# Two attention mixers of a float32 transformer stack: attention steps ahead of the weight splits, and a new close of the output projection

## Time and profile before

| What | Value |
|---|---|
| Median of three runs | 1328.12 us (1325.83 to 1328.39) |
| The profiled execution's own time | 1326.24 us |
| Its span, first to last instruction | 1324.4 us |
| TensorE matmul busy | 1219.8 us, 92% |
| TensorE weight load busy | 1071.9 us, 81% |
| VectorE busy | 847.3 us, 64% |
| ScalarE busy | 574.4 us, 43% |
| GpSimd busy | 44.6 us, 3% |
| Mean granted TensorE clock | 0.939 of full |
| Loaded from memory | 243.06 MB, 187 GB/s over the span |

### The profile page before, as it was taken

One profiled execution on the slowest core, in us unless ns is written; L12 is line 12 of the kernel. 1 busy time (PEld: TensorE's weight loads), 2 busy tenths in 40 slices (PEclk: granted clock), 3 DMA queues, 4 the chain that ended last, 5 costly groups with the idle time before them and its releaser, 6 DMA issues.

```text
span 1324.4 us, 18386 instructions
## 1 busy us (share of the span) xinstructions
PE 1219.8 (92%) x7598; PEld 1071.9 (81%) x7598; DVE 847.3 (64%) x1276; ACT 574.4 (43%) x837; POOL 44.6 (3%) x86
## 2 busy tenths in 40 slices
PE   4989998999999988789999957999999899899997
PEld 3984776899998867579999847999988697899996
DVE  5662544587777766668777765977776445655554
ACT  5302231554444544455444455444446443744442
POOL 1010000000000000000000000000001100000000
PEclk9998556999999998899999978999999999899999
DMA  7933010488776423238877603977755432265530
GB/s 286 205 122 128 35 63 30 150 306 323 281 278 223 187 96 128 96 122 321 332 278 278 217 28 157 363 282 280 283 190 193 141 141 99 99 236 186 185 139 32
DMA packets 35746, 248.96 MB, mean 188 GB/s; under 512 B 4272, under 2 KB 4288, under 8 KB 6608
## 3 DMA queue, kind: packets, MB, share of 16 engines
q1 hardware_dynamic: 26352, 189.13, 38.3%
q0 software_dynamic: 9168, 57.56, 12.7%
q10 hardware_dynamic: 144, 1.11, 0.2%
HBM read 243.06 MB, written 4.19 MB: 187 GB/s over the span
## 4 chain that ended last, share of the span: by engine, by line
PE 81%; DVE 11%; ACT 4%; issue 2%; DMA 1%; DVEq 0%; SPq 0%; ACTq 0%
PE bank L1143 68%; DVE wlo L598 3%; PE bank L1318 2%; ACT whi L366 1%; PE bank L1502 1%; PE bank L1332 1%; DMA raw<-in_stream 1%; PE bank L1374 1%; DVE x L616 1%; DVE work L614 1%; PE bank L1221 1%; DVE ul L643 1%; PE bank L1385 1%; PE bank L1339 1%; PE bank L1341 1%
## 5 line engine op out<-in xcount | busy, mean ns | idle before, releaser
L598 DVE TENSOR_TENSOR wlo<-raw,whi 128x2048 fp32r<-128x2048 f32 x175 | 398.7, 2283 | 133.1 <-ACT whi L366 133.0
L1143 PE MATMUL bank<-uh,whi 128*128 128x256 f32 x1280 | 370.6, 289 | 2.9 <-DVE ul L643 2.9
L1143 PE MATMUL bank<-ul,whi 128*128 128x256 f32 x1280 | 363.6, 284 | 0.0
L1143 PE MATMUL bank<-uh,wlo 128*128 128x256 f32 x1280 | 363.5, 284 | 0.0
L366 ACT ACTIVATE whi<-raw 128x2048 fp32r<-128x2048 f32 x175 | 332.4, 1906 | 71.3 <-PE bank L1143 62.3
L1143 PEld LDWEIGHTS bank<-uh,whi 128*128 128x128 f32 x1280 | 246.9, 193 | 11.0 <-issue 8.9
L1143 PEld LDWEIGHTS bank<-ul,whi 128*128 128x128 f32 x1280 | 247.0, 193 | 4.7 <-issue 2.6
L1143 PEld LDWEIGHTS bank<-uh,wlo 128*128 128x128 f32 x1280 | 246.8, 193 | 0.0
L1143 PE MATMUL bank<-whi,hh 128*128 128x512 f32 x544 | 214.9, 395 | 0.0
L1143 PE MATMUL bank<-wlo,hh 128*128 128x512 f32 x544 | 212.9, 391 | 0.0
L1143 PE MATMUL bank<-whi,hl 128*128 128x512 f32 x544 | 212.2, 390 | 0.0
(11 more groups left out here) (229 smaller groups left out, 1157.8 us busy)
## 6 DMA issues: line engine op xcount, KB each, us to landing
raw<-in_stream SPq DMA_DIRECT2D x178, 1024.0 KB, 4.9
qk<-in_w_mod POOLq DMA_DIRECT2D x48, 1024.0 KB, 6.0
bias_rows<-PT POOLq DMA_DIRECT2D x1, 3072.0 KB, 36.3
u<-bias_rows POOLq DMA_DIRECT2D x16, 128.0 KB, 2.5
con<-in_con ACTq DMA_DIRECT2D x1, 1083.5 KB, 6.9
x<-in_x SPq DMA_DIRECT2D x2, 512.0 KB, 8.3
vo<-in_fin_g POOLq DMA_DIRECT2D x2, 512.0 KB, 4.3
out_y<-vo SPq DMA_DIRECT2D x2, 512.0 KB, 2.6
```

The costliest lines, as they stand in the source:

```text
L598: nc.vector.tensor_tensor(wlo[:, c % RING, 0:w], raw[:, raw_index(c) % RING, 0:w], whi[:, c % RING, 0:w].bitcast(fp32), ALU.subtract).then ...
L1143: ins = mm(out, st, mv, start=start and i == 0, stop=stop and i == 2, skip_group_check=True)
```

## The change

- The step tables are now separate for the two phases, and most steps sit in other quarters. Phase d has one turn for each pair and a table `JOIN_AT` for `combine`.
- On ScalarE, in both phases, `hi_upto` moves from q = 0, ahead of the attention work, to q = 1, behind it.
- In phase d the copy of the turned block to `PT` moves from VectorE to ScalarE, always into PT[:, 0].
- The value chunks 6 and 7 are no longer run as one: each takes both tiles in its own turn (`rows_of_values`), waits only for its own weights and raises `used` at its end.
- In `project_beside`, chunk 14 runs tile 0 with its steps 0 and 1, then the steps 2 and 3 without matmuls between; then chunk 15 closes tile 0, chunk 14 runs tile 1, `norm(e, 0)`, and chunk 15 closes tile 1.

The tables:

```diff
+SCORE_AT = {"d": {(4, 3): 0, (5, 2): 1, (6, 3): 2, (7, 2): 3, (10, 3): 4, (11, 1): 5, (12, 3): 6, (13, 1): 7},
+            "b": {(4, 1): 0, (4, 3): 1, (6, 1): 2, (6, 3): 3, (10, 1): 4, (10, 3): 5, (12, 1): 6, (12, 3): 7}}
+JOIN_AT = {(5, 3): 0, (6, 2): 1, (7, 3): 2, (8, 2): 3, (11, 2): 4, (12, 0): 5, (13, 2): 6, (14, 0): 7}
+TURN_AT = {"d": {(6, 1): (0, 0), (7, 0): (1, 0), (8, 1): (2, 0), (9, 0): (3, 0),
+                 (11, 3): (4, 0), (12, 1): (5, 0), (13, 3): (6, 0), (14, 1): (7, 0)},
+           "b": {(5, 1): (0, 0), (5, 2): (0, 1), (5, 3): (1, 0), (6, 0): (1, 1), (7, 1): (2, 0), (7, 2): (2, 1),
+                 (7, 3): (3, 0), (8, 0): (3, 1), (11, 1): (4, 0), (11, 2): (4, 1), (11, 3): (5, 0), (12, 0): (5, 1),
+                 (13, 1): (6, 0), (13, 2): (6, 1), (13, 3): (7, 0), (14, 0): (7, 1)}}
+VALUE_AT = {"d": {(6, 3): 0, (7, 2): 1, (9, 0): 2, (9, 2): 3, (12, 0): 4, (12, 2): 5, (14, 0): 6, (14, 2): 7},
+            "b": {(5, 3): 0, (6, 1): 1, (7, 3): 2, (8, 1): 3, (11, 3): 4, (12, 1): 5, (13, 3): 6, (14, 1): 7}}
+OUT_AT = {"d": {(8, 1): 0, (10, 1): 1, (13, 2): 2, (14, 3): 3},
+          "b": {(6, 3): 0, (8, 3): 1, (12, 3): 2, (14, 3): 3}}
```

ScalarE in phase d, and behind the second "..." in phase b:

```diff
             for i, q in QUARTERS:
-                if q == 0:
-                    if i and i <= 12 and MIXER[i - 1][0] == "v" and MIXER[i - 1][2] == 1:
-                        value_copies(MIXER[i - 1][1], 0, DIFF + i - 1, d_v)
-                    hi_upto(min(DIFF + i + 3, MLP1 + 1))
+                if q == 0 and 1 <= i <= 12 and MIXER[i - 1][0] == "v" and MIXER[i - 1][2] == 1:
+                    value_copies(MIXER[i - 1][1], 0, DIFF + i - 1, d_v)
+                if (i, q) in TURN_AT["d"]:
+                    p = TURN_AT["d"][i, q][0]
+                    act.wait_ge(s_tr["d"], p + 1)
+                    if p >= 1:
+                        act.wait_ge(s_pv["d"], p)
+                    nc.scalar.activation(PT[:, 0, :], bank[5][:, 0:384], ACT.Copy).then_inc(s_pt["d"], 1)
...
+                if q == 1:
+                    hi_upto(min(DIFF + i + 3, MLP1 + 1))
...
-                if q == 0:
+                if (i, q) in SCORE_AT["b"]:
+                    pair_exps("b", SCORE_AT["b"][i, q])
+                if (i, q) in OUT_AT["b"]:
+                    pair_upper(2, OUT_AT["b"][i, q], one)
+                if q == 1:
                     hi_upto(min(MOBA + i + 3, MLP3 + 1))
```

VectorE in phase d:

```diff
-                if (i, q) in TURN_AT and TURN_AT[i, q][1] == 0:
-                    turned_copy("d", *TURN_AT[i, q])
+                if (i, q) in JOIN_AT:
+                    combine(JOIN_AT[i, q])
...
-                if (i, q - 2) in SCORE_AT or (i - 1, q + 2) in SCORE_AT:
-                    combine(SCORE_AT.get((i, q - 2), SCORE_AT.get((i - 1, q + 2))))
```

TensorE, in `project_beside` and in the loops over `MIXER`:

```diff
-                for c in range(3):
+                for c in range(2):
                     pe.wait_ge(lo_ready, m0 + c + 1)
                     pe.wait_ge(ol_ready, 4 * r + c + 1)
                     add_rows(m0 + c, e, *parts(c), c == 0, False, steps=lambda q: steps(c, q))
+                pe.wait_ge(lo_ready, m0 + 3)
+                pe.wait_ge(ol_ready, 4 * r + 3)
+                add_rows(m0 + 2, e, *parts(2), False, False, (0,), steps=lambda q: steps(2, q))
+
+                for q in (2, 3):
+                    steps(2, q)
                 pe.wait_ge(lo_ready, m0 + 4)
                 pe.wait_ge(ol_ready, 4 * r + 4)
-                add_rows(m0 + 3, e, *parts(3), False, True)
+                add_rows(m0 + 3, e, *parts(3), False, True, (0,))
+                add_rows(m0 + 2, e, *parts(2), False, False, (1,))
                 norm(e, 0)
+                add_rows(m0 + 3, e, *parts(3), False, True, (1,))
...
+            def rows_of_values(m, g, steps):
+
+                pe.wait_ge(lo_ready, m + 1)
+                for t in range(NT):
+                    ins = half_values(m, g, t, None, lambda t, q: steps(2 * t + q % 2))
+                ins.then_inc(used, 1)
...
-                elif kind == "v" and k == 0:
-                    pe.wait_ge(d_add, 3)
-                    both_halves(DIFF + i, None, lambda t, q, i=i: (beside("d", 1, i + t)(q), dswap(i + t, q)))
+                elif kind == "v" and j == 1:
+                    if k == 0:
+                        pe.wait_ge(d_add, 3)
+                    rows_of_values(DIFF + i, k, steps)
```

More of the change, by code:

```diff
@@ L498, in value_copies @@
                 for t in range(NT):
-                    if t == 0:
-                        act.wait_ge(v_ps, base + h + 1)
+                    if t == 0 and h == 0:
+                        act.wait_ge(v_ps, base + 1)
                     else:
@@ L565, in _ @@
                     elif k == 1:
-                        value_copies(j, 2, MOBA + i - 1, b_v)
+                        value_copies(j, 1, MOBA + i - 1, b_v)
                         if i == 2:
                             spread_copy(3, cb, 6)
-                if q == 0:
+                if (i, q) in SCORE_AT["b"]:
[3 more added lines that the diff above has]
+                if q == 1:
                     hi_upto(min(MOBA + i + 3, MLP3 + 1))
[L571 to L574, removed]
             act.wait_ge(mod_ready, 3)
@@ L735, in turned_copy @@
             def turned_copy(ph, p, c):
-                n = p if ph == "d" else 2 * p + c
+                n = 2 * p + c
                 dve.wait_ge(s_tr[ph], n + 1)
@@ L1043, in _ @@
                     rope_sum(qk[:, 2 * j:2 * j + 2, :], bank[k], 2, r).then_inc(d_add, 1)
[L1044 to L1051 removed]
+                if (i, q) in SCORE_AT["d"]:
+                    pair_maxima("d", SCORE_AT["d"][i, q])
+                if (i, q) in JOIN_AT:
+                    combine(JOIN_AT[i, q])
+                if (i, q) in VALUE_AT["d"] and VALUE_AT["d"][i, q] % 2:
+                    sub_norm(VALUE_AT["d"][i, q] // 2)
+                if (i, q) in OUT_AT["d"]:
+                    pair_lower(1, OUT_AT["d"][i, q], lam[:, 6:7])
                 if q == 1:
                     lo_upto(min(DIFF + i + 3, MLP1 + 1))
[L1054 to L1055 removed]
             add_and_norm(3)
@@ L1103, in _ @@
             for i, q in QUARTERS:
[L1104 to L1109, removed]
+                if (i, q) in TURN_AT["b"]:
+                    turned_copy("b", *TURN_AT["b"][i, q])
+                if (i, q) in SCORE_AT["b"]:
+                    pair_maxima("b", SCORE_AT["b"][i, q])
+                if (i, q) in VALUE_AT["b"] and VALUE_AT["b"][i, q] % 2:
+                    j = VALUE_AT["b"][i, q] // 2
                     dve.wait_ge(s_exp["b"], 4 * j + 4)
@@ L1118, in _ @@
                     ins.then_inc(o_sc, 1)
-                if (i, q) in OUT_AT:
-                    pair_lower(2, OUT_AT[i, q], one)
+                if (i, q) in OUT_AT["b"]:
+                    pair_lower(2, OUT_AT["b"][i, q], one)
                 if q == 1:
@@ L1416, in steps @@
                 def steps(q):
[L1417 to L1424, removed]
+                    if (i, q) in VALUE_AT[ph]:
+                        pair_values(ph, r, VALUE_AT[ph][i, q])
+                    if (i, q) in TURN_AT[ph]:
+                        pair_turn(ph, *TURN_AT[ph][i, q])
+                    if (i, q) in SCORE_AT[ph]:
+                        pair_scores(ph, SCORE_AT[ph][i, q])
+                    if (i, q) in OUT_AT[ph]:
+                        pair_out(r, OUT_AT[ph][i, q])
                 return steps
@@ L1579, in both_halves @@
                     for g in range(2):
-                        ins = half_values(m + g, g, t, None if e is None else ul_no(e, t), steps)
+                        ins = half_values(m + g, g, t, ul_no(e, t))
                         if t == 1:
@@ L1584, in both_halves @@
                             ins.then_inc(v_ps, 1)
-                        if e is not None and t == 0 and g == 0:
+                        if t == 0 and g == 0:
                             norm(e, 1)
@@ L1645, in _ @@
                     spread_col(mod[:, 64:72], 6)
-                elif kind == "v" and k == 0:
-                    pe.wait_ge(b_copied, 3)
-                    both_halves(MOBA + i, None, lambda t, q, i=i: beside("b", 2, i + t)(q))
+                elif kind == "v" and j == 1:
+                    if k == 0:
+                        pe.wait_ge(b_copied, 3)
+                    rows_of_values(MOBA + i, k, beside("b", 2, i))
                 elif kind == "f":
```

20 lines of the change are left out of this document (7 added, 13 removed).

## The result

The kernel after takes 1346.65 us (median of 4 runs, 1344.71 to 1347.33), the kernel before 1328.2 us on the same chip: a ratio of 1.0141 with a 95% interval of 1.0123 to 1.0158. It is slower by 18.5 us, where 17.9 were forecast (1346 against 1328.12). The profiled execution took 1346.7 us, with a span of 1344.9 us and a mean granted clock of 0.934 [before: 0.939].

The account below looks back on a forecast made before the run. Bound by TensorE except where it waits for VectorE or ScalarE. 1326.24 us + 8.3 lost in d (terms 9.3 before overlaps) + 9.5 in b = 1344.0; the median runs 1.9 higher, so 1346 us, range 1333 to 1354.

Parts of the forecast that it names:

- Scores 2: Phase d, quarter (6,3): waits 1.2 us for the rotary sum of chunk 5, behind lower and upper split 9.
- turn 2: Phase d, (8,1): stalls 5.5 us for `combine` 2, behind split 10, maxima 3, exponentials 3 and the norm of output 0.
- Scores 4: Phase d: 1.7 us of stall ahead, for the rotary sum of chunk 9, behind split 13.
- Turn 4: Phase d: stalls 4.8 us instead of 2.13, behind exponentials 5, split 14, rotary sum 10 and `combine` 4; 2.6 us lost.
- Quarter (12,2): Phase d: waits for the rotary sum of chunk 11, stalls of 0.6 and 3.2 us plus the clock; 5.0 us lost.
- slow stretch: TensorE at 1.2 GHz of 2.4 behind a stall: 1.6 us charged for a stall over 3 us.
- Turn 6: Phase d, (13,3): stalls 4.6 us where 5.15 stood; 0.3 us gained.
- The end: Phase d, last out step: stalls of 5.3 and 1.6 us instead of 1.81 and 0.27; chunk 15 begins 6.8 us later.
- values 0: Phase b, (5,3): wait 4.1 us where 0.66 was lost; 3.3 us lost and 1.6 of clock.
- values 4: Phase b, chunk 11: come at 1095.6 instead of 1091.08; 3.3 us lost and 1.6 of clock.
- The close at nothing: Closing the output projection by tile costs nothing; 2.7 us gained for each mixer only if the last out step were ready.
- The table loads: Phase d, ScalarE: 6 remain of 8, 2.6 us less, counted as nothing; rival that they pay in full, chance 0.04.

Follow-up runs that it names:

- e1: Kernel before with only ScalarE's upper split moved behind the attention work (q = 1) in both phases: 1356.37 us, ratio 1.0211.
- e2: Kernel after with only ScalarE's upper split put back ahead of the attention work (q = 0) in both phases: 1309.47 us, ratio 0.9856.
- e3: Kernel after with the old close of the output projection (chunk 14 whole, then chunk 15 whole): 1346.53 us, ratio 1.0138.
- e7: e2 with the old close of the output projection: 1309.31 us, ratio 0.9872.
- e5: Kernel after with the upper split put back to q = 0 in phase d only: 1323.61 us, ratio 0.9975.
- e9: e2 with VectorE's lower split moved from q = 1 to q = 3 in phase b only: 1306.18 us, ratio 0.9841.
- e6: Kernel after with the copy of the turned block in phase d back on VectorE: 1335.17 us, ratio 1.0066.

## Why the prediction was right

The mechanism is the forecast's: the upper split behind the exponentials holds the lower split, and this holds `combine` in d and the turned copy in b. e1 and e2 show it from both sides. Step by step, in phase d:

- **Scores 2 and turn 2.** Scores 2 waited 1.03 us (1.2 said). Turn 2 waited 3.14 us and not 5.5. TensorE came when I said; `combine` 2 came earlier. This is the largest single error of the walk, 2.4 us: the term was the chain from split 10 through maxima, exponentials and the norm of output 0. With the 3.9 us by which phase d began later taken off, lower split 10 ended at 491.7 (492.9 said), exponentials 3 at 494.1 (496.1) and the norm at 497.1 (499.3), so half of the error arose up to the split and most of the rest between maxima and exponentials.
- **Scores 4**: 1.78 us (1.7). **Turn 4**: 4.55 (4.8). **Quarter (12,2)**: 3.06 (3.2), but the clock stayed at full speed behind it, where I had charged a slow stretch. **Turn 6**: 4.46 (4.6).
- **The end**: 4.88 and 1.66 us (5.3 and 1.6). Counted from the start of the phase, chunk 15 came 3.9 us later than before where I said 6.8; the turn explains 2.4 us of the difference. Behind it 2.3 us more were lost, 1.6 said. Phase d cost 6.3 us, 8.3 said.

In phase b: values 0 waited 3.78 us (4.1), pair 2 waited 2.22 and 0.87 (2.4 and 1.7), values 4 3.77 (4.3), chunk 13 2.25 and 1.34 (2.6 and 1.7). Each of these waits was shorter than the walk had it, yet the phase cost 10.1 us, 9.5 said: idle up to chunk 15 was 16.2 us and not 19, and the busy time grew more than I charged. The waits were taken a little too long and the slow clock too cheap, and the two errors nearly cancel. In d idle up to chunk 15 was 25.4 us, 29 said.

So 16.3 us arise in the phases where I said 17.8, and the medians differ by 18.5. The total is closer than its terms, and that is luck: in b the waits and the clock were off in opposite directions, and what lies outside the phases, which no part of the forecast covers, happened to fill the gap. The terms of d add to 9.3 us and those of b to 9.7, and I used 8.3 and 9.5; no row shows the overlap of 1.0 us that I took off in d. The walk was right in which step waits and for whom at every wait over 3 us, with sizes within 0.6 us but for turn 2. The sizes of the slow clock were not: in e1 they put me off by more than the waits did (some 7 us against 2), in e2 I had both too small.

The close at nothing holds for the totals (e3 and e7), but in d it costs some 1.7 us, and the 2.7 us for each mixer that it was to give with a ready out step did not come in phase b of e2. The table loads: phase d has 6 where it had 8. The load of 1.28 us ahead of the Sqrt of output 0 ran beside VectorE's reduction, as the forecast said, and ended 0.2 us after VectorE had its result (499.71). ScalarE's timeline of the kernel after:

```profile
498.03 0.58 ACT L536 ACTIVATE u<-bank 128x512 f32<-128x512 f32 x1
498.62 1.28 ACT L538 ACT_TABLE_LOAD   x1
499.92 0.21 ACT L538 ACTIVATE msq<-msq 128x4 f32<-128x4 f32 x1
```

The load starts 0.01 us behind the activation ahead of it and ends 0.02 us ahead of the next. The drain that the Trainium skill (ScalarE: Activation LUTs, What ACT_TABLE_LOAD costs) adds to a load doesn't appear in this trace, so the rows' price was the right one to take. No run here changes the loads alone.

## What to carry to other kernels

In a kernel whose engines run a fixed order, put a long piece of work (here ScalarE's split of 1.9 us) ahead of the short steps that wait for another engine, if its input is there: behind them it takes over their waits and hands them to everything queued behind it. It is no rule for every engine: VectorE's lower split moved behind the short steps gained 4.0 us in phase b, and lost 2.0 in d. So place each engine's long piece phase by phase, after asking what short work with a waiting reader starts at that quarter. And take a change apart into its parts: here one call's place hid a gain of 18 us.

## What the runs showed of the hardware

**Like waits, unlike clocks.** Windows of the kernel after behind three waits, of 3.14, 3.06 and 3.77 us:

```profile
502.29:505.50 3.21, 3.21 (x15) 3.21 (x16) 0.70 (x1) 1.91 (x3) 0.00 (x0) 0.50 0.00 0
...
551.74:555.00 3.26, 3.26 (x21) 2.39 (x22) 1.16 (x4) 2.25 (x4) 0.00 (x0) 1.00 0.85 307
...
1106.40:1112.50 6.10, 6.09 (x29) 6.09 (x30) 0.56 (x1) 0.03 (x1) 0.00 (x0) 0.50 0.45 172
```

The first and the last ran at 1.2 GHz, for at least 3.2 and 6.1 us, and the middle one at 2.4 GHz, though its wait was as long as the first. So a single slow stretch can't be priced from the length of the wait ahead of it; over whole phases the busy time shows it, 8.3 us between e2 and the kernel after in the two phases together.

**Unchanged code, another length.** Phase d begins between 438.25 and 443.34 us of the span in the twelve profiles, though the code ahead is the same. Of the 3.9 us in the kernel after, 1.8 come from one stretch of 48 matmuls in the first mixer, which took 7.06 us there and 5.29 us before, at a granted clock of 0.73 instead of 1.00, and more from its neighbours. The chain that ended last, first before, then after:

```profile
37.68 5.29 PE bank L1143 x48
```

```profile
38.06 7.06 PE bank L1153 x48
```

The Trainium skill (TensorE: Matmul & The Clock Gate, What's actually happening) says of the ramp at the start of a kernel that its number of slow matmuls differs from run to run, and that the ramp costs less than 1% of a typical span. The spread here, 5.1 us or 0.4%, is as small, but of the 3.9 us between before and after only 0.4 us arises in the first 37 us. The stretch between the two phases, unchanged too, took from 410.0 to 412.9 us in the twelve profiles. A phase itself repeats better where its code is the same: d took 134.5, 134.6 and 134.6 us in e2, e5 and e9, b 149.8, 149.2 and 149.2 in after, e5 and e6. For a change worth 10 us the spread of the rest is a third to a half of it: compare phases between fixed marks, and medians, and not the totals of two profiles.
